# Mixture-of-experts stages of a long fp32 kernel: the gather of tokens moves between the two halves of the gate product

## What is computed

```python
scores = jax.nn.sigmoid((xt @ router_w).astype(F32))        # 16 experts in 4 groups
...
top_group = jnp.argmax(grp_score, axis=-1)                  # one group of 4 for each token
_, idx = lax.top_k(jnp.where(in_group, sel, -jnp.inf), TOP_K)
...
h = jax.nn.silu(jnp.einsum('td,edf->etf', xt, w1)) * jnp.einsum('td,edf->etf', xt, w3)
h = h * gates.T[:, :, None].astype(h.dtype)
y = jnp.einsum('etf,efd->td', h, w2)
...
ple = (p[i] @ ple_w_proj[i]) * jax.nn.sigmoid(x @ ple_w_gate[i])
x = layer_norm(DEEPNORM_ALPHA * x + ffn + ple, ln_ffn_g[i], ln_ffn_b[i])
```

## Time and profile before

| | |
|---|---|
| median of 3 runs | 2049.3 us (2048.67 to 2050.21) |
| the profiled execution, its own time | 2053.41 us |
| its span, first to last instruction | 2051.6 us |
| mean granted clock of TensorE | 0.991 |
| TensorE busy | 2003.3 us, 98% |
| VectorE busy | 1462.2 us, 71% |
| ScalarE busy | 1209.3 us, 59% |

### The profile page before, as it was taken

The page is one execution under the profiler, slowest core; times in us unless marked ns, Lnnn a source line. Parts: engine busy times, 40 slices in busy tenths (PEclk is TensorE's granted clock), DMA queues, the critical chain, the costliest instruction groups (busy, mean ns, idle before and its releaser), DMA issues.

```text
span 2051.6 us, 28253 instructions
## 1 busy us (share of the span) xinstructions
PE 2003.3 (98%) x10490; PEld 1685.1 (82%) x10490; DVE 1462.2 (71%) x1995; ACT 1209.3 (59%) x1693; POOL 3.2 (0%) x10
## 2 busy tenths in 40 slices
PE   8999999999999999989999999999999999999999
PEld 5678888879787888879888899888877888998887
DVE  7878999884678999987664579754576555675554
ACT  4448888764657888764444468644486544545442
POOL 0000000000000000000000000000000000000000
PEclk9999999999999999999999999999999999999999
DMA  7448999965237999965565545655533655465553
GB/s 266 154 165 315 363 351 356 365 248 195 83 127 276 355 361 353 358 261 197 166 207 190 194 136 175 226 183 187 185 113 124 213 185 190 152 201 189 190 179 103
DMA packets 124120, 453.21 MB, mean 221 GB/s; under 512 B 14032, under 2 KB 14160, under 8 KB 123216
## 3 DMA queue, kind: packets, MB, share of 16 engines
q1 hardware_dynamic: 122976, 446.01, 62.6%
q0 software_dynamic: 720, 5.24, 0.7%
q10 hardware_dynamic: 288, 0.16, 0.0%
HBM read 450.31 MB, written 1.05 MB: 220 GB/s over the span
## 4 chain that ended last, share of the span: by engine, by line
PE 88%; DVE 7%; ACT 2%; issue 1%; DMA 1%; SPq 0%; DVEq 0%; ACTq 0%
PE bank L341 15%; PE bank L342 15%; PE bank L343 15%; PE bank L1214 10%; PE bank L1215 10%; PE bank L1217 4%; PE bank L334 3%; PE bank L335 3%; PE bank L336 3%; DVE w_lo L314 3%; PE bank L695 1%; PE bank L2697 1%; DMA raw<-in_stream 1%; PE bank L462 1%; PE bank L2813 1%
## 5 line engine op out<-in xcount | busy, mean ns | idle before, releaser
L314 DVE TENSOR_TENSOR w_lo<-raw,w_hi 128x1024 fp32r<-128x1024 f32 x824 | 981.2, 1221 | 406.3 <-ACT w_hi L307 403.0
L307 ACT ACTIVATE w_hi<-raw 128x1024 fp32r<-128x1024 f32 x824 | 851.4, 1056 | 570.2 <-PE bank L343 348.6
L341 PE MATMUL bank<-w_hi,x_hi 128*128 128x512 f32 (+1 forms) x832 | 327.7, 394 | 3.4 <-DVE scr L1086 1.7
L342 PE MATMUL bank<-w_lo,x_hi 128*128 128x512 f32 (+1 forms) x832 | 324.6, 390 | 0.0
L343 PE MATMUL bank<-w_hi,x_lo 128*128 128x512 f32 (+1 forms) x832 | 324.4, 390 | 0.0
L341 PE MATMUL bank<-w_hi,c_hi 128*128 128x512 f32 x570 | 223.1, 391 | 3.3 <-issue 2.1
L343 PE MATMUL bank<-w_hi,c_lo 128*128 128x512 f32 x570 | 221.9, 389 | 0.0
L342 PE MATMUL bank<-w_lo,c_hi 128*128 128x512 f32 x570 | 221.8, 389 | 0.0
L334 PE MATMUL bank<-x_hi,w_hi 128*128 128x256 f32 x672 | 191.2, 285 | 1.0 <-DVE w_lo L314 1.0
L335 PE MATMUL bank<-x_lo,w_hi 128*128 128x256 f32 x672 | 190.4, 283 | 0.0
L336 PE MATMUL bank<-x_hi,w_lo 128*128 128x256 f32 x672 | 190.3, 283 | 0.0
(11 more groups left out here) (476 smaller groups left out, 2546.8 us busy)
## 6 DMA issues: line engine op xcount, KB each, us to landing
raw<-in_stream SPq DMA_DIRECT2D x838, 512.0 KB, 4.7
ln_rows<-in_ln POOLq DMA_DIRECT2D x4, 1024.0 KB, 4.8
scr<-in_s SPq DMA_DIRECT2D x3, 512.0 KB, 8.4
w_room<-in_window SPq DMA_DIRECT2D x1, 1024.0 KB, 16.6
x<-in_x POOLq DMA_DIRECT2D x1, 1024.0 KB, 6.7
out_x<-x SPq DMA_DIRECT2D x4, 256.0 KB, 2.3
par<-in_par SPq DMA_DIRECT2D x1, 812.0 KB, 13.4
x_room<-in_xt SPq DMA_DIRECT2D x2, 256.0 KB, 4.6
```

The costliest lines, as they stand in the source:

```text
L307: nc.scalar.activation(w_hi[:, n % RING, :], raw[:, n % RING, :], ACT.Copy).then_inc(hi_done, 1)
L314: nc.vector.tensor_tensor(w_lo[:, n % RING, :], raw[:, n % RING, :], w_hi[:, n % RING, :].bitcast(F32), ALU.subtract).then_inc(lo_done, 1)
L341: nc.tensor.matmul(out, xh, hi, start=start, stop=False)
L342: nc.tensor.matmul(out, xh, lo, start=False, stop=False)
```

## The change

The gather moves ahead of the second half of the gate product, and the ranks one part forward. The gather makes one product a chunk over all 448 slots (`SLOTS` is 448), with four accumulating matmuls each, 32 in all. Each chunk lies in one bank, from which ScalarE makes two copies and VectorE two subtractions. The gathered rows get buffers of their own, `own_hi` and `own_lo`, because `x_hi` and `x_lo` are still read by the second half; the experts' first hidden values go to `x_hi` and `x_lo` instead of `h_first`. The products with the gates and the transposes become `turn_slots_pe` and stay behind the second half, in other banks. The doubled narrow columns that they need are written later, as `twice`. VectorE's list is put in a new order, with all ten tiles' splits still in it, and two parts of the embedding are made before the experts. The table `numbers` (448 columns) replaces three tables of 261 columns. `routing` leaves the shared scratch, and `h_whole`, `h_twin`, `h_single` and `y_parts` name the new places.

```diff
@@ moe_pe
-                    if half == 0 and part == 2:
+                    if half == 0 and part == 1:
                         ranks_pe(pe, st)
-            gather_pe(pe, st)
+                if half == 0:
+                    gather_pe(pe, st)
+            turn_slots_pe(pe, st)
@@ moe_act
             tanh_of_gate(0)
+            for k in range(KC):
+                act.wait_ge(pe_did["gathered"], pe_did.at("gathered", st, k))
+                nc.scalar.activation(own_hi[:, k, :], Q[k % 4][:, 0:T], ACT.Copy).then_inc(...)
+                nc.scalar.activation(xg[:, k, :, 0:NARROW], narrow(Q[k % 4]), ACT.Copy).then_inc(...)
+            split_hi(act)
             split_hi(act)
             tanh_of_gate(1)
             for i in range(3):
...
-            split_hi(act)
-            for i in range(4):
...
-            for k in range(KC):
...
@@ gather_pe
             pe.wait_ge(dve_did["slots"], dve_did.at("slots", st))
...
+            pe.wait_ge(dve_did["x_lo"], dve_did.at("x_lo", st, "rows", TT - 1))
             for k in range(KC):
                 b = Q[k % 4]
                 before(pe, b)
                 for tt in range(TT):
                     for part in (x_rows_hi, x_rows_lo):
...
+                        last = nc.tensor.matmul(b[:, 0:SLOTS], part[:, tt, k * P:(k + 1) * P], slots_r[:, tt, :], ...
+                after(b, ("dve", ("xg_lo", st, k, "narrow")))
+        def turn_slots_pe(pe, st):
+            before(pe, Q[2])
+            pe.wait_ge(dve_did["slots"], dve_did.at("slots", st, "twice"))
+            pe.wait_ge(dve_did["gates"], dve_did.at("gates", st, "by slot"))
...
+            after(Q[2], ("dve", ("xg_lo", st, "gates")))
+            for i in range(3):
+                b = Q[(3, 2, 3)[i]]
+                before(pe, b)
...
+                after(b, ("act", ("xg_hi", st, "turned", i)))
@@ moe_dve
             split_lo(dve)
             gates = route_dve(dve, st)
-            split_lo(dve)
-            slots_dve(dve, st)
-            split_lo(dve)
-            gates()
             for tt in range(TT):
...
+            slot = slots_dve(dve, st)
+            split_lo(dve, 1)
+            for k in range(KC):
+                if k == 4:
+                    split_lo(dve, 1)
+                dve.wait_ge(act_did["xg_hi"], act_did.at("xg_hi", st, k, "narrow"))
+                nc.vector.tensor_tensor(own_lo[:, k, :], Q[k % 4][:, 0:T], own_hi[:, k, :].bitcast(F32), ALU.subtract)
+                nc.vector.tensor_tensor(xg[:, k, :, NARROW:P], narrow(Q[k % 4]), xg[:, k, :, 0:NARROW].bitcast(F32), ALU.subtract)
+            split_lo(dve)
+            gates()
+            for tt in range(TT):
...
+            ple_part(dve, st, 0, 0)
+            split_lo(dve)
+            ple_part(dve, st, 1, 0)
             split_lo(dve)
             dve.wait_ge(pe_did["gathered"], pe_did.at("gathered", st, "gates"))
-            nc.vector.tensor_copy(slot_gate, Q[0][:, 0:4 * PLACES])
...
+            nc.vector.tensor_copy(slot_gate, Q[2][:, 0:4 * PLACES])
@@ slots_dve
-            v(nc.vector.tensor_tensor(offset, ...))
             for tt in range(TT):
-                for j in range(PLACES):
...
+                last = nc.vector.tensor_scalar(slots_r[:, tt, :], column("numbers", 0, SLOTS), slot[:, tt:tt + 1], None, ALU.is_equal)
@@ experts_dve
-            ple_part(dve, st, 0, 0)
...
-                if j in (1, 2, 3):
-                    ple_part(dve, st, *divmod(j, 2))
+                if j in (0, 1):
+                    ple_part(dve, st, j, 1)
```

More of the change, by code:

```diff
@@ L945, in gather_pe @@
         def gather_pe(pe, st):
-            before(pe, Q[0])
             pe.wait_ge(dve_did["slots"], dve_did.at("slots", st))
-            pe.wait_ge(dve_did["gates"], dve_did.at("gates", st, "by slot"))
-            gate4 = routing[:, 392:400].rearrange("p (t e) -> p t e", t=TT)
-            for j in range(PLACES):
[L951 to L974, removed]
+            pe.wait_ge(dve_did["x_lo"], dve_did.at("x_lo", st, "rows", TT - 1))
             for k in range(KC):
@@ L979, in gather_pe, with slots_of @@
                     for part in (x_rows_hi, x_rows_lo):
-                        last = nc.tensor.matmul(narrow(b), part[:, tt, k * P:(k + 1) * P],
-                                                slots_r[:, tt, T:SLOTS].rearrange("p (s t) -> p s t", t=P)[:, :, 0:NARROW],
+                        last = nc.tensor.matmul(b[:, 0:SLOTS], part[:, tt, k * P:(k + 1) * P], slots_r[:, tt, :],
                                                 start=tt == 0 and part is x_rows_hi, stop=tt == TT - 1 and part is x_rows_lo)
-                last.then_inc(pe_did["gathered"], pe_did.next("gathered", st, 4 + k))
-                after(b, ("dve", ("xg_lo", st, 4 + k)))
+                last.then_inc(pe_did["gathered"], pe_did.next("gathered", st, k))
+                after(b, ("dve", ("xg_lo", st, k, "narrow")))
+        def slots_of(place, tt):
+            if place < WHOLE:
+                return slots[:, tt, place * P:(place + 1) * P]
+            return twice[:, tt, (place - WHOLE) * P:(place - WHOLE + 1) * P]
+        def turn_slots_pe(pe, st):
+            before(pe, Q[2])
+            pe.wait_ge(dve_did["slots"], dve_did.at("slots", st, "twice"))
+            pe.wait_ge(dve_did["gates"], dve_did.at("gates", st, "by slot"))
+            gate4 = routing[:, 392:400].rearrange("p (t e) -> p t e", t=TT)
+            for j in range(PLACES):
+                for tt in range(TT):
+                    last = nc.tensor.matmul(Q[2][:, 4 * j:4 * j + 4], slots_of(j, tt), gate4[:, tt, :],
+                                            start=tt == 0, stop=tt == TT - 1, skip_group_check=True)
+            last.then_inc(pe_did["gathered"], pe_did.next("gathered", st, "gates"))
+            after(Q[2], ("dve", ("xg_lo", st, "gates")))
+            for i in range(3):
+                b = Q[(3, 2, 3)[i]]
+                before(pe, b)
+                for j in range(2 * i, min(2 * i + 2, PLACES)):
+                    for tt in range(TT):
+                        last = nc.tensor.transpose(bank(b)[:, j % 2, tokens(tt)], slots_of(j, tt), column("ident", 0, P))
+                last.then_inc(pe_did["gathered"], pe_did.next("gathered", st, "turned", i))
+                after(b, ("act", ("xg_hi", st, "turned", i)))
         def router_act(act):
@@ new lines, in moe_dve @@
+            split_lo(dve)
+            gates()
+            for tt in range(TT):
+                numbers = column("numbers", WHOLE * P, REST).rearrange("p (s n) -> p s n", n=NARROW).unsqueeze(2).to_broadcast([P, HALVES, 2, NARROW])
+                last = nc.vector.tensor_scalar(twice_r[:, tt, :].rearrange("p (s i n) -> p s i n", s=HALVES, i=2), numbers, slot[:, tt:tt + 1],
+                                               None, ALU.is_equal)
+            last.then_inc(dve_did["slots"], dve_did.next("slots", st, "twice"))
@@ L1033, in moe_dve @@
[L1033 to L1036, removed]
+            nc.vector.tensor_copy(slot_gate, Q[2][:, 0:4 * PLACES]).then_inc(dve_did["xg_lo"], dve_did.next("xg_lo", st, "gates"))
         slot_gate = norm[:, 42:42 + 4 * PLACES]
@@ L3363 @@
     row("ring_if_three", [np.zeros(3), at[0] - at[2]])
-    row("place_base", [0, P, *base])
-    put("iota", np.tile(np.arange(P, dtype=np.float32)[None], (P, 1)))
-    put("iota_twice", np.tile(np.arange(P, dtype=np.float32)[None] % NARROW, (P, 1)))
+    row("numbers", np.arange(SLOTS))
     put("ident", np.eye(P, dtype=np.float32))
```

70 lines of the change are left out of this document (34 added, 36 removed).

## The result

The changed kernel takes **2055.4 us** (median of 11 runs, 2053.5 to 2057.5) against 2050.2 us of the kernel before (11 runs beside it, 2048.7 to 2053.3). The ratio is 1.0024 with a 95% interval of 1.0016 to 1.0031: slower by 0.24%, where 2046.1 was forecast. The profiled execution has a span of 2053.3 us and an own time of 2055.1, close to its median. The profiled execution of the kernel before was 3.2 us above the median given here (2053.4 against 2050.2), so the two spans are only 1.7 us apart where the medians are 5.2 apart.

What follows compares the result with a forecast made beforehand. TensorE, busy 2003 of 2051.6 us, was taken as the bound. Per mixture, -1.0 earlier start, -2.5 gather, +1.7 new wait and +0.2 clock make -1.6, so -3.2 for two: 2049.3 to 2046.1 us, range 2041.9 to 2049.4.

Steps and rivals of the forecast that it cites:

- The new buffers for gathered rows change addresses, not sizes of operands: Buffers for the gathered rows: only their addresses change, so no time was charged for them.
- The wider table of constants: Load at the start: 187 more columns, 96 KB, 0.4 us, beside other loads while TensorE waits for the first tile only.
- The ranks and the slots: Ahead of the gather: ranks one part (2.75 us) earlier, slots ready at 120.4, the 0.87 us wait gone.
- The gather: On TensorE: 32 matmuls of 448 columns at 0.202 us, 6.5 us in all instead of 8.96, so -2.5.
- The chunks: Gathered chunks leave TensorE every 0.8 us, ScalarE and VectorE keep up, and the second gate half starts at 127.3.
- The new wait: Inside the ten transposes: TensorE waits 1.7 us for VectorE's late copy of the gates out of bank 2.
- The gap: In front of the experts: 3.64 us between matmul starts, taken as six register loads from `order`, left unchanged.
- The clock: Half clock at the experts' start: a longer thin stretch, 1.4 us lost instead of 1.2, so +0.2 a mixture.
- A: Rival: the gate copy does not hold TensorE; each mixture gets -3.8 + 0.2, giving 2042.1 us; chance 0.18.
- B: Rival: the long thin stretch costs more clock, +1.2 to +1.5 a mixture, giving 2048.5 to 2049.1 us; chance 0.13.
- C: Rival: VectorE's queue runs late before the gate copy; 3.9 us late is +2.3 a mixture, 2053.9 us; chance 0.07.
- D: Rival: the experts' loads become the limit and the gain is lost, giving 2049.3 us; chance 0.02.

Runs made afterwards that it cites:

- after_128: The changed kernel with 96 bytes of unused padding per partition, so the buffers behind it start at a multiple of 128 bytes; 2045.88 us.
- before_128: The kernel before with 64 bytes of unused padding per partition, so the buffers behind it start at a multiple of 128 bytes; 2049.07 us.
- ranks_late: after_128 with the ranks put back behind the third part of the first gate half, as in the kernel before; 2052.2 us.
- banks_310: after_128 with the slot-matrix transposes in banks 3, 1, 0 instead of 3, 2, 3, so none needs the gates' bank; 2039.4 us.
- weights_32: before_128 with the split weights w_hi and w_lo starting 32 bytes beyond a multiple of 128, all other buffers at one; 2088.3 us.
- loads_before: before_128 with the six register loads moved, two at a time, behind the first three parts of the second gate half; 2038.1 us.

## Why the prediction was wrong

The step that failed is the sentence "The new buffers for gathered rows change addresses, not sizes of operands", and with it "The wider table of constants (187 columns, 96 KB, 0.4 us at the 240 GB/s of rows 7)", which priced the table's load and not its place. Both were costed at nothing. What they cost: after is 9.0 to 9.5 us slower than after_128, which does the same work with these buffers at a multiple of 128. Part of that, 0.7 to 1.4, the kernel before paid too (before against before_128, not clear of the noise), so the term that the forecast lacks is about 8 us. At equal placement the change gives 2049.07 - 2045.88 = 3.2 us (2.7 by the ratios), where 3.2 was forecast. Agreement to the tenth is chance: the runs of each spread over 4 to 5 us, and two terms inside were off in opposite directions.

Step by step, first mixture:

- *The ranks and the slots.* Forecast: ranks read from 115.2 on, slots at 120.4, no wait. Measured: from 114.76, the last compare ended at 119.97, and the gather started at 120.12 without a pause; the 0.87 went. ranks_late shows what it would be otherwise.
- *The gather.* 0.206 us for 448 columns (0.203 in after_128) against 0.202; 6.6 us against 6.5.
- *The chunks.* The first four come out of VectorE 0.82 apart, in step with TensorE (0.8 was forecast), the last four 0.60 apart. The second half starts at 126.82, forecast 127.3; both halves start 0.5 earlier than in the trace of before, and the rest of the difference is nothing.
- *The new wait.* 1.2 us inside the transposes, released by the copy into `norm`; forecast 1.7. The copy came at 141.57, inside the bounds that I had given (141 to 144.5).
- *The gap.* It was the register loads, as assumed, but not of fixed length: 2.8 instead of 3.4. In all the stage is 2.5 us shorter, where 1.8 was forecast.
- *The clock.* This term was too small: 12 expert matmuls at half clock and not 7 or 8, +0.8 instead of +0.2. The window of 2.8 us in the earlier trace rows ends before the seventh of them does, so the spell before was priced at 1.2 where it had cost 1.5. The gate matmuls, transposes and pauses now stand in one row (137.8 to 146.1), and the granted clock is at 0.50 in one stretch of 10.2 us (140.8 to 151.1), where it was two of 3.4. The stage came out 0.7 better and the clock 0.6 worse: -1.7 a mixture against -1.6.

**The rivals.** A: the copy did hold TensorE; with it out of the way (banks_310) the kernel gains 6.5 us, where A's figure is 4.0 below the forecast. A's -3.8 does not follow from the prediction's own terms either: -1.0 and -2.5 make -3.5. B: came half true; the clock cost 0.6 more than the forecast's 0.2, where B has 1.2 to 1.5 more. C: VectorE was on time in all steps; the slower time has nothing to do with its queue. D: no such wait shows; TensorE's only listed wait for a load in the whole run is that for the first tile. The slower result came from something that was in none of the four. Nor did the signs that were named catch it: the copy came inside its bounds and no wait appeared in front of the gather.

## What to carry to other kernels

A change of one buffer's width moves every buffer behind it: work out where the operands of the big matmuls start, before and after, and try padding them to a multiple of 128 bytes per partition (it paid here for 512 columns; 256-column matmuls were no faster for it). When TensorE is busy for longer with fewer instructions and nothing waits, compare the mean of one matmul by operand name, not by line. And what stands in front of a gap on the engine's own queue (here six register loads) may be its cause even where the profile names another engine; it is worth more if it can go behind long matmuls, since the clock comes back with it.

## What the runs showed of the hardware

- **The start of an operand sets the step of a 128x512 matmul,** for this kernel's 32-bit operands, back to back, at full clock. Held operand: 227 ns at a multiple of 128 bytes per partition, 229 at 64 beyond, 233 at 32 beyond. Moving operand: 227 to 228, 233 to 234 at 64 beyond (the scatter), 234 at 32 beyond (weights_32). With only the weights 32 beyond, the whole kernel is 1.9% slower (weights_32 against before_128). Matmuls of 256 columns, with the roles swapped, took 120 ns at a multiple and with the held weights 32 beyond, and 116 to 117 with the moving x 32 beyond. Why stays open. What both operands of one matmul shifted would cost was not measured, and 96 beyond a multiple was not tried.
- The Trainium skill ("SBUF — State Buffer", Operand start alignment) asks only that an operand start at a multiple of its element's size, and says of this: "This is about legality, not speed". The runs here agree that all these starts are legal; in speed they differ, by the figures above.
- The Trainium skill ("TensorE: Matmul & The Clock Gate", "Step-by-step: what each phase is for") works out 216 ns from start to start for 512 columns. None of this kernel's groups of such matmuls shows it; the lowest median is 227.
- **Six register loads from SBUF on TensorE's queue left gaps of 2.2 to 3.4 us** when they stood between short matmuls and the experts (banks_310, before), and none in front of the experts when they were issued behind long matmuls (loads_before).
